# The softmax division moved behind the value products, from ss to the head outputs, in a one-core decoder step

## What is computed

```python
def _attend(q, k, v, cum_q, cum_kT, q_pos):
    s = jnp.einsum("bqhd,bkhd->bhqk", q, k).astype(jnp.float32) * ATTN_SCALE
    s = s + jnp.swapaxes(cum_q, 1, 2)[..., None] - cum_kT[:, :, None, :]
    k_pos = jnp.arange(k.shape[1])
    s = jnp.where(k_pos[None, :] <= q_pos[:, None], s, -jnp.inf)
    p = jax.nn.softmax(s, axis=-1).astype(v.dtype)
    return jnp.einsum("bhqk,bkhd->bqhd", p, v)
```

## Time and profile before

| | |
|---|---|
| median of 3 runs | 2908.66 us (2902.79 to 2909.69) |
| the profiled execution, its own time | 2906.83 us |
| its span, first to last instruction | 2905.2 us |
| mean granted clock of PE | 0.955 of full |
| busy: PE, DVE, ACT, POOL | 93%, 38%, 27%, 33% of the span |
| HBM read and written | 182.43 MB, 41.26 MB |

### The profile page before, as it was taken

How to read it: one execution, slowest core, us unless ns; L and a number is a source line. 1 busy time by engine, 2 the same in 40 slices (tenths; PEclk the granted TensorE clock), 3 DMA queues, 4 the chain that set the end, 5 groups by cost and what they waited for, 6 DMA issues and landing times.

```text
span 2905.2 us, 44679 instructions
## 1 busy us (share of the span) xinstructions
PE 2696.3 (93%) x16907; PEld 2605.1 (90%) x16907; DVE 1109.6 (38%) x2082; ACT 784.1 (27%) x1431; POOL 951.4 (33%) x546
## 2 busy tenths in 40 slices
PE   8999969999999999689997899889799999999994
PEld 8999959999999999579996778779599999999993
DVE  3222362422222222762354555552642222222237
ACT  2111134111111111252223555551511111111114
POOL 2212143112111122352323878843512212112114
PEclk9999969999999999899998989989899999999997
DMA  3111101111111111024688555631011111111111
GB/s 111 44 51 43 45 22 37 47 49 44 45 44 44 53 50 44 23 80 144 197 286 270 143 168 152 179 111 44 22 44 52 44 52 45 44 52 45 44 37 59
DMA packets 203054, 225.87 MB, mean 78 GB/s; under 512 B 13223, under 2 KB 168871, under 8 KB 201884
## 3 DMA queue, kind: packets, MB, share of 16 engines
q1 hardware_dynamic: 194748, 190.40, 21.5%
q0 software_dynamic: 8160, 33.30, 3.7%
HBM read 182.43 MB, written 41.26 MB: 77 GB/s over the span
## 4 chain that ended last, share of the span: by engine, by line
PE 79%; DVE 7%; POOL 4%; issue 4%; DMA 3%; ACT 2%; SPq 1%; POOLq 0%; DVEq 0%; ACTq 0%
PE ps L1746 24%; PE ps L1747 24%; PE ps L1748 24%; POOL ss L830 2%; PE ps L2012 2%; DVE ln_t L1405 1%; DVE ln_t L1409 1%; PE ps L2042 1%; DVE ln_d L1350 1%; PE ps L1997 1%; PE ps L1994 1%; DMA ncb<-ccum 1%; DMA o_t<-oe 1%; PE ps L2029 1%; PE ps L2028 1%
## 5 line engine op out<-in xcount | busy, mean ns | idle before, releaser
L1746 PE MATMUL ps<-xh,whi 128*128 128x344 f32 x3288 | 1068.0, 325 | 31.5 <-POOL xl L711 18.4
L1747 PE MATMUL ps<-xl,whi 128*128 128x344 f32 x3288 | 1055.2, 321 | 0.0
L1748 PE MATMUL ps<-xh,wlo 128*128 128x344 f32 x3288 | 1055.0, 321 | 0.0
L664 POOL TENSOR_TENSOR wlo<-wraw,whi 128x1024 fp32r<-128x1024 f32 x197 | 471.2, 2397 | 1659.0 <-ACT whi L890 1658.9
L1746 PEld LDWEIGHTS ps<-xh,whi 128*128 128x128 f32 x3288 | 620.7, 189 | 59.5 <-POOL xl L711 34.6
L1748 PEld LDWEIGHTS ps<-xh,wlo 128*128 128x128 f32 x3288 | 622.3, 189 | 0.0
L1747 PEld LDWEIGHTS ps<-xl,whi 128*128 128x128 f32 x3288 | 622.1, 189 | 0.0
L890 ACT ACTIVATE whi<-wraw 128x1024 fp32r<-128x1024 f32 x197 | 208.2, 1058 | 1116.9 <-DMA wraw<-ffn_w_gu 649.3
L1746 PE MATMUL ps<-zh,whi 128*128 128x344 f32 x1440 | 465.7, 323 | 17.6 <-DVE x L1477 9.4
L1747 PE MATMUL ps<-zl,whi 128*128 128x344 f32 x1440 | 464.1, 322 | 0.0
L1748 PE MATMUL ps<-zh,wlo 128*128 128x344 f32 x1440 | 462.1, 321 | 0.0
(11 more groups left out here) (209 smaller groups left out, 2384.3 us busy)
## 6 DMA issues: line engine op xcount, KB each, us to landing
wraw<-ffn_w_gu SPq DMA_DIRECT2D x88, 512.0 KB, 3.9
wraw<-ffn_w_down SPq DMA_DIRECT2D x44, 512.0 KB, 3.5
kp<-cache_k SPq DMA_DIRECT2D x32, 512.0 KB, 5.5
vp<-cache_v SPq DMA_DIRECT2D x32, 512.0 KB, 4.1
wraw<-a_w_in SPq DMA_DIRECT2D x24, 512.0 KB, 3.7
wraw<-kv_w SPq DMA_DIRECT2D x16, 512.0 KB, 4.3
q_t<-hl POOLq DMA_DIRECT2D x8, 1024.0 KB, 4.6
v_t<-vst POOLq DMA_DIRECT2D x8, 1024.0 KB, 6.9
```

The costliest lines, as they stand in the source:

```text
L664: pool.tensor_tensor(narrow(wlo[:, s, :], cols), narrow(wraw[:, s, :], cols), f32(narrow(whi[:, s, :], cols)), ALU.subtract).then_inc(w_lo, 1)
L1746: pe.matmul(out, w_h, m_h, start=start, stop=False)
L1747: pe.matmul(out, w_h, m_l, start=False, stop=False)
L1748: return pe.matmul(out, w_l, m_h, start=False, stop=stop)
```

## The change

The softmax division is taken off POOL's `norm` on ss. `turn` now waits for the exps alone. `inverse` runs once a head (two buffers of rs and ri), SP stores the 1024 reciprocals of a head to r_t in HBM (`store_sums`, element by element, transposed) and reads them back as one row for all 128 partitions into rb (`load_sums`). POOL multiplies the whole oe of a head, 128x1024, by rb (`scale`), and `store_head` waits for that. The last pair multiplies ost by rlast on DVE. `o_take` moves from ACT to DVE. The lists of SP and POOL are put into a new order. The list of SP for a pair is now: page 2, next_qk(b, 1), page 3, next_v(b, 0), store_sums(b, 1), store_head(b, 0), load_sums(b, 1), pages 0 and 1 of the next pair, next_v(b, 1), next_qk(b+1, 0), store_sums(b+1, 0), store_head(b, 1), load_sums(b+1, 0).

```diff
@@ -166,8 +166,8 @@
-        rs = ma.put("rs", [P, STEPS, 2], F32)
-        ri = ma.put("ri", [P, STEPS, 2], F32)
+        rs = ma.put("rs", [P, 2, STEPS, 2], F32)
+        ri = ma.put("ri", [P, 2, STEPS, 2], F32)
@@ -264,6 +264,8 @@
+        rb = [Area(PAGES_AT - 3 * D * 4 + e * TP * 4).put(f"rb{e}", [P, TP], F32) for e in range(2)]
+        rlast = Area(XH_AT + 5 * TP * 4).put("rlast", [P, TP], F32)
@@ -283,6 +285,7 @@
+        r_t = nc.dram_tensor("r_t", [H, TP], F32, kind="Internal").ap()
@@ -337,9 +340,11 @@
-              ("khi", "klo", "sfull", "sdr", "exp", "rinv", "pnorm", "tfull", "pthi", "ptlo", "ofull", "ohalf", "odone")}
+              ("khi", "klo", "sfull", "sdr", "exp", "rinv", "omul", "onorm", "tfull", "pthi", "ptlo", "ofull", "ohalf", "odone")}
...
+        r_st = [sem(f"r_st{e}") for e in range(2)]
+        r_in = [sem(f"r_in{e}") for e in range(2)]
@@ -561,11 +566,28 @@
             for g in range(2):
...
+            sp.wait_ge(kv["s3dma"], 16 * 2)
...
+            def store_sums(b, e):
...
+                inverted = sp.to_reg(2 * b + e + 1 + 2) if not isinstance(b, int) else 2 * b + e + 1 + 2
...
+                sp.wait_ge(at["rinv"], inverted)
+                sp.dma_start(r_t[bass.ds(2 * b + e, 1), :].rearrange("a (n p) -> p (a n)", p=P),
+                             ri[:, e, :, :].rearrange("p j t -> p (j t)"), allow_slow_non_contiguous=True).then_inc(r_st[e], 16)
...
+            def load_sums(b, e):
...
+                stored_sums = sp.to_reg(16 * (b + 2)) if not isinstance(b, int) else 16 * (b + 2)
...
+                sp.wait_ge(r_st[e], stored_sums)
+                sp.dma_start(rb[e][:, :], r_t[bass.ds(2 * b + e, 1), :].to_broadcast([P, TP])).then_inc(r_in[e], 16)
...
             def store_head(b, e):
...
+                scaled = sp.to_reg(2 * b + e + 1)
...
-                sp.wait_ge(at["odone"], PAIR * b + STEPS * (e + 1) + 2)
+                sp.wait_ge(at["omul"], scaled)
@@ -583,20 +605,40 @@
-            with sp.Fori(0, KB - 1) as b:
-                next_qk(b, 0)
+            def pair(b, last=False):
...
+                next_qk(b, 1)
...
-                next_qk(b, 1)
...
+                store_sums(b, 1)
...
+                load_sums(b, 1)
...
+                if not last:
+                    next_qk(b + 1, 0)
+                store_sums(b + 1, 0)
...
+                if not last:
+                    load_sums(b + 1, 0)
...
+            next_qk(0, 0)
+            store_sums(0, 0)
+            load_sums(0, 0)
+            with sp.Fori(0, KB - 2) as b:
+                pair(b)
+            pair(KB - 2, True)
...
+            store_sums(KB - 1, 1)
+            sp.wait_ge(at["ofull"], PAIR * (KB - 1) + STEPS)
+            for e in range(2):
+                sp.wait_ge(r_st[e], 16 * (KB + 1))
+                sp.dma_start(rlast[e * DH:(e + 1) * DH, :],
+                             r_t[2 * KB - 2 + e:2 * KB - 1 + e, :].to_broadcast([DH, TP])).then_inc(r_in[0], 16)
@@ -820,15 +862,15 @@
-            def norm(b, st):
...
-                j = st % STEPS
-                inverted = pool.to_reg(PAIR * b + st + 1) if not isinstance(b, int) else PAIR * b + st + 1
+            def scale(b, e):
...
+                summed = pool.to_reg(PAIR * b + STEPS * (e + 1) + 2)
...
-                pool.wait_ge(at["rinv"], inverted)
-                for t in range(2):
-                    pool.tensor_scalar(ss[j][:, t, 0:span(st, t)], ss[j][:, t, 0:span(st, t)], ri[:, j, t:t + 1], None,
-                                       ALU.mult).then_inc(at["pnorm"], 1)
+                pool.wait_ge(at["odone"], summed)
+                loaded = pool.to_reg(16 * (b + 1))
...
+                pool.wait_ge(r_in[e], loaded)
+                pool.tensor_tensor(oe[e][:, :], oe[e][:, :], rb[e][:, :], ALU.mult).then_inc(at["omul"], 1)
...
             def add_halves(b, e):
@@ -839,26 +881,24 @@
-            norm(0, 0)
...
-            for st in range(1, STEPS):
-                norm(0, st)
             for m in range(WR):
...
-            with pool.Fori(0, KB - 1) as b:
-                norm(b, STEPS)
-                k_split(b + 1, 0)
-                for st in range(STEPS + 1, PAIR):
-                    norm(b, st)
+            def pair(b, last=False):
...
+                k_split(b + 1, 1)
+                scale(b, 0)
...
-                norm(b, PAIR)
-                k_split(b + 1, 1)
-                for st in range(PAIR + 1, PAIR + STEPS):
-                    norm(b, st)
+                if not last:
+                    k_split(b + 2, 0)
+                scale(b, 1)
...
-            for st in range(STEPS, PAIR):
-                norm(KB - 1, st)
...
+            k_split(1, 0)
+            with pool.Fori(0, KB - 2) as b:
+                pair(b)
+            pair(KB - 2, True)
@@ -1171,8 +1211,12 @@
+                e = st // STEPS % 2
+                if j == 0 and t == 0:
...
+                    act.wait_ge(at["rinv"], 2 * (b + st // PAIR) + e + 1)
...
-                               accum_out=rs[:, j, t:t + 1]).then_inc(at["exp"], 1)
+                               accum_out=rs[:, e, j, t:t + 1]).then_inc(at["exp"], 1)
...
             def pt_high(b, st, g):
@@ -1180,18 +1224,6 @@
-            def o_take(b, st):
...
-                e, j = st // STEPS % 2, st % STEPS
-                act.wait_ge(at["ofull"], PAIR * b + st + 1)
-                if j == 0:
...
-                    act.wait_ge(oe_add[e], 16 * (b + st // PAIR + 1))
-                if st == 1:
...
-                    act.wait_ge(sm["osum"], b + 1)
-                act.activation(oe[e][:, j * 2 * P:(j + 1) * 2 * P], ps[:, 6 + st % 2, 0:2 * P], ACT.Copy).then_inc(at["odone"], 1)
...
             def o_half(st):
@@ -1208,8 +1240,6 @@
-                elif st >= 2:
-                    o_take(b, st - 2)
@@ -1247,7 +1277,7 @@
             for m in range(3, KB - 1):
...
-            act.wait_ge(at["odone"], 2 + PAIR * KB)
+            act.wait_ge(at["onorm"], 1)
@@ -1270,6 +1300,7 @@
         def _(dve):
...
             for n, (s, credit) in enumerate(((ffn[0]["sum"], DBANKS), (ffn[0]["down"], 1), (at["ptlo"], 2), (at["odone"], 2),
+                                             (at["rinv"], 2), (r_st[0], 16), (r_st[1], 16),
@@ -1642,9 +1673,15 @@
             def inverse(b, st):
-                j = st % STEPS
-                dve.wait_ge(at["exp"], 2 * (PAIR * b + st) + 2)
-                dve.reciprocal(ri[:, j, :], rs[:, j, :]).then_inc(at["rinv"], 1)
...
+                e = st // STEPS % 2
+                stored_sums = dve.to_reg(16 * (b + st // PAIR + 1)) if not isinstance(b, int) else 16 * (b + st // PAIR + 1)
...
+                dve.wait_ge(r_st[e], stored_sums)
+                summed = dve.to_reg(2 * (PAIR * b + st) + 2) if not isinstance(b, int) else 2 * (PAIR * b + st) + 2
...
+                dve.wait_ge(at["exp"], summed)
+                dve.reciprocal(ri[:, e, :, :], rs[:, e, :, :]).then_inc(at["rinv"], 1)
...
             def pt_low(b, st, g):
@@ -1664,6 +1701,19 @@
+            def o_take(b, st):
...
+                e, j = st // STEPS % 2, st % STEPS
+                if j == 0:
...
+                    added = dve.to_reg(16 * (b + st // PAIR + 1)) if not isinstance(b, int) else 16 * (b + st // PAIR + 1)
...
+                    dve.wait_ge(oe_add[e], added)
+                valued = dve.to_reg(PAIR * b + st + 1) if not isinstance(b, int) else PAIR * b + st + 1
...
+                dve.wait_ge(at["ofull"], valued)
+                dve.tensor_copy(oe[e][:, j * 2 * P:(j + 1) * 2 * P], ps[:, 6 + st % 2, 0:2 * P]).then_inc(at["odone"], 1)
...
             def step(b, st, last=False):
@@ -1672,18 +1722,18 @@
-                if not (last and st + 2 >= PAIR):
+                if (st + 2) % STEPS == STEPS - 1 and not (last and st + 2 >= PAIR):
...
+                elif st >= 2:
+                    o_take(b, st - 2)
...
             def sample_sum(b):
...
-                taken = dve.to_reg(2 + PAIR * (b + 1)) if not isinstance(b, int) else 1 + PAIR * (b + 1)
-                dve.wait_ge(at["odone"], taken)
                 for t in range(2):
@@ -1694,8 +1744,6 @@
             for st in range(3):
                 for t in range(2):
...
-            for st in range(2):
-                inverse(0, st)
             for st in range(2):
...
             with dve.Fori(0, KB - 1) as b:
@@ -1720,8 +1768,10 @@
             for m in range(3, KB - 1):
-                if m == 5:
+                if m == 3:
...
+                    dve.wait_ge(r_in[0], 16 * (KB + 1))
+                    dve.tensor_tensor(ost[:, :], ost[:, :], rlast[:, :], ALU.mult).then_inc(at["onorm"], 1)
@@ -2004,7 +2054,7 @@
-                    pe.wait_ge(at["pnorm"], 2 * s + 2)
+                    pe.wait_ge(at["exp"], 2 * s + 2)
...
```

(39 more changed lines are left out.)

## The result

| | before | changed |
|---|---|---|
| median of the runs side by side | 2907.89 us | 2933.65 us (2921.05 to 2937.02) |
| ratio to before, 95% interval | | 1.0084 (1.0050 to 1.0117) |
| profiled execution | 2906.83 us, span 2905.2 | 2921.05 us, span 2919.4 |
| period of a pair in the attention | 43.8 us | 46.2 us |
| POOL busy over the span | 33% | 26% |

The account below looks back on a forecast made before the run. POOL's list, waits included, was taken as the bound at 43.8 us a pair. Six periods of 38.4 give 32 us less, first pair 13 less, last pair +3: together -42, predicting 2866 us, range 2845 to 2891.

Parts of the forecast that it names:

- The period of PE's own list, 38.4 us: Attention loop: without the norm, PE's list with ACT and DVE latencies sets the pace, 38.4 us a pair for 43.8.
- Part "Queues", "Cost 0": SP's new order: page 2, asked for after `scale`, and the loads behind it still come in time; cost 0.
- `store_sums` at 3 us: SP's store of a head's 1024 sums, 4 B each, taken at 3 us from stores of equal count.
- "Both lie where nothing waits for them": `store_sums` and `load_sums` on SP: reciprocals are taken two steps early and `scale` comes late, so nothing waits.
- The loop of `oe_add`, rival 2: DVE's `o_take` waits through store and `add_halves`; this loop binds at 41.5 us a pair, 2889 us; chance 0.22.
- Rival 4: Slower: 4-B elements on q1 make the DMA engines the bound, deciding from 109 ns a packet; 2943 us, chance 0.04.
- "r_t landing after 10 us": Sign of slow 4-B elements: the DMA of r_t lands after 10 us.
- "DMA share at 0.9": Sign that the DMA engines are the bound through 4-B elements: their share at 0.9.
- "wrong altogether": Sign: PE waits for pages or keys once a pair, meaning SP's list, held at `store_sums` or `store_head`, loads late.
- First pair -13: First pair of the attention: scores no longer behind norms, 13 us less.
- Last pair +3: Last pair: longer chain to the first `o_sum` +4, rlast product on DVE +1, norm waits gone -2; +3 us.
- `o_take` on DVE, 0.4 us and 0 on the chain: Copy of output halves on DVE: 0.4 us each, 8 a pair, behind the maxima, so 0 on the chain.

Follow-up runs that it names:

- x_mid: x_both with POOL's split of the next keys put between the scale and the add; 2873.6 us, ratio 0.9886 to the kernel before.
- x_both: Changed kernel with POOL scaling and adding before it splits the next keys, and sums stored in 128 pieces of 32 bytes; 2876.2 us, ratio 0.9899.
- x_wide: Changed kernel with the sums of a head stored as 128 pieces of 32 bytes instead of 1024 of 4; 2920.8 us, ratio 1.0051.
- x_oldq: Changed kernel with sums in 32-byte pieces and SP's and POOL's order of the kernel before; 2876.7 us, ratio 0.9904.
- x_mid_el: Changed kernel with only POOL's order edited to scale, split, add, sums still in 4-byte elements; 2928.9 us, ratio 1.0081.
- x_piece8: x_both with the sums stored as 512 pieces of 8 bytes instead of 128 of 32; 2875.6 us, ratio 0.9890.
- x_pool: Changed kernel with only POOL's order edited: scale and add before the split of the next keys; 2929.5 us, ratio 1.0082.
- x_bstore: Kernel before plus a store of 1024 4-byte elements ahead of each head's store on SP; 2998.8 us, ratio 1.0309.
- x_act: Changed kernel with the copy of the output halves out of PSUM back on ScalarE; 2934.2 us, ratio 1.0108.
- x_both_act: x_both with the copy of the output halves back on ScalarE; 2876.4 us, ratio 0.9890.
- x_oldq_el: Changed kernel with only SP's and POOL's order put back as before, sums still in 4-byte elements; 2933.2 us, ratio 1.0089.

## Why the prediction was wrong

- **The period of PE's own list, 38.4 us: right, but not reached.** Where both rings are gone the period is 38.8 (x_mid) and 39.05 (x_both), the clock 0.99 to 1.00 (I had asked for 0.96 or more), and the scores still wait up to 1.1 us for the maxima. The changed kernel never came down to it, as the rings hold it at 46.2.
- **Part "Queues", "Cost 0": the step that failed.** I followed the chain from a page over five issues, the landing and `k_split` to `scale` and to page 2, found page 2 in time, and stopped. It had to be closed: behind `scale` SP issues again the keys on which the next `scale` waits. From `store_head` to the first issue of the keys SP's list takes 3.6 us in one head (1649.04 to 1652.60) and 5.8 in the other (1669.50 to 1675.26). With my own terms behind that, 3.1, 6.2, 3.6 and 2.4, the closed chain is 18.9 and 21.1 us, 40.0 a pair against 38.4: over the period before any landing is late. And the keys of the burst that follows each store land later than 6.2 (8.2 in the changed kernel, 9.2 in x_wide, up to 12.5 in single heads of its chain). x_oldq against x_wide prices it: 44 us.
- **`store_sums` at 3 us: mis-sized by five.** In the loop of x_mid_el it lands after 14.3 to 18.5 us, in the changed kernel's after 12.2 to 13.8 where the chain has it, and at the end of the changed kernel, with little beside it, after about 8. My upper bound was 11.9, from the average packet of q1, and it was nearer than the value I took from one store of equal count but 64 bytes, which POOL had issued and not SP. The Trainium skill, DMA: Bandwidth & Descriptors, Rules for kernel authors, says that a strided last dimension becomes one descriptor per element: the trace agrees, as 16 x 1024 of the 16896 more packets under 512 B are these elements, and x_wide, which has 128 pieces a head, has 16 x 896 fewer. The Trainium skill, DMA: Bandwidth & Descriptors, Bandwidth, by whose figure for a small packet I had estimated 10.8 us, was closer than my row: from 128 pieces (x_both) to 512 (x_piece8) the landing grew 3.3 us, 8.6 ns a piece, and to the 1024 of x_pool, where `load_sums` is issued 13.2 to 15.1 us after the store, by 4 to 6, 8 to 11 ns a piece.
- **"Both lie where nothing waits for them": wrong for SP.** The data were not needed sooner. But `load_sums` waits for the landing inside a list in which pages and keys stand behind it, and o_t's store lands behind the elements. x_bstore shows the second by itself.
- **The loop of `oe_add`, rival 2.** DVE did wait for it (11.9 us in the window), as a consequence of the late stores, as I read it; in x_both and x_mid that wait isn't among those listed. Not the cause.
- **Rival 4** had the right suspect and the wrong mechanism. It "decides from 109 ns a packet" of engine time; a head has 0.77 x 23.5 = 18.1 us of it in x_mid_el and 0.77 x 19.5 = 15.0 in x_both, for 56 more pieces an engine, so by this estimate a piece takes an engine some 3.1 / 56 = 55 ns. What decided was the landing, in two in-order lists. Its sign "r_t landing after 10 us" came true, and "DMA share at 0.9" did not (0.67). Of "wrong altogether", PE waiting for pages came true (L2092, 13.2 us).
- **First pair -13: right** (-12.3), in the one execution that has a trace; x_act, with the same order of SP and POOL, has -5.7. **Last pair +3: +10.4**, by the elements: x_wide's takes 39.0 us. In x_mid the first `o_sum` waits 7.3 us.
- **`o_take` on DVE, 0.4 us and 0 on the chain: right**, 0.418 us measured, and x_act and x_both_act show no cost. **`scale` 2.4 us: right**, 2.38.

With both taken out, x_mid's 2873.6 stands 8 us above the forecast of 2866. The terms against the spans: the first pair gives 8.4 us and not 13, the six periods 30.0 and not 32, the last pair costs 0.8 and not 3, and 2.1 more lie behind it: 35.5 less in all, for 42.

## What to carry to other kernels

When a step is moved between in-order queues, close every loop: from the moved instruction through each queue that it waits in, until the same instruction of the next turn, and compare that length, landings under load included, with the period. When an edit that should help does nothing, look in its trace for a second bound of the same height before the theory is dropped; two edits, of which neither alone moved the period of the loop, were worth 57 us together. A mean busy share doesn't settle whether an engine limits: look at it in windows of a few us inside the wait. A small transfer is priced by its pieces and by what stands behind it, in the issuing list and among the transfers, not by its bytes or by whether its data are urgent.

## What the runs showed of the hardware

- 4 KB stored by SP as 1024 elements of 4 bytes took 14.3 to 18.5 us to landing in the loop of x_mid_el and 12.2 to 13.8 in the changed kernel's chain, 512 pieces of 8 bytes 9.3, 128 of 32 bytes 6.0 (3.8 in x_oldq and 8.8 in x_wide, by the same 128 pieces). The 1024 pieces of 64 bytes of the earlier trace rows took 2.7, issued by POOL; whether the size of the piece, its place in HBM, the load beside it or the issuing engine makes the difference no run separates.
- The landing of an element store came 5.6 us after the DMA engines had fallen nearly idle (share 0.06 from 1719.00 to 1724.60 in x_mid_el).
- A store issued by SP right behind it (0.65 us after) took longer to issue: 4.10 us at 1710.14 in x_mid_el, median 3.1 over its 14, 0.55 in the changed kernel, where 11 to 16 us lie between the two.
- A read of the second operand with a stride of 32 bytes cost POOL's `scale` 2.9 to 3.2 us in place of 2.4, hidden in x_both; with a stride of 8 bytes, in x_piece8, it took 2.4.
- The mean busy share of the DMA engines didn't tell fast from slow: 0.78 in x_mid (2873.6 us) and 0.78 in x_oldq_el (2933.2), 0.67 in the changed kernel.
